# The first layer's down GEMM in a two-block kernel: four of its eight weight panels in three fp32r passes instead of fp32

## What is computed

```python
def rmsnorm(x, g):
    xf = x.astype(jnp.float32)
    y = xf * lax.rsqrt(jnp.mean(xf * xf, axis=-1, keepdims=True) + EPS)
    return (y * g.astype(jnp.float32)).astype(x.dtype)

def modulate_2(x, g, shift, scale):
    return rmsnorm(x, g) * (1 + scale) + shift

def conv_ffn(h, w_up, conv_w, conv_b, w_down, rows):
    u = h @ w_up
    ...                                   # depthwise convolution of u
    a, g = jnp.split(u, 2, axis=-1)
    return (jax.nn.silu(g) * a) @ w_down

# in second_block, for each layer:
mod_l = (jax.nn.silu(c) @ mod_w[layer] + mod_b[layer])[:, None, :]
...
xl = xl + g2l * conv_ffn(hl, ffn_w_up[layer], ffn_conv_w[layer], ffn_conv_b[layer], ffn_w_down[layer], rows)
xc = xc + g2c * conv_ffn(hc, ffn_w_up[layer], ffn_conv_w[layer], ffn_conv_b[layer], ffn_w_down[layer], None)
```

## Time and profile before

| | us |
|---|---|
| median of three runs | 2857.93 (2853.77 to 2861.48) |
| the profiled execution | 2861.58 |
| span of the profile | 2859.8 |
| PE busy | 2674.9 (94%) |
| DVE busy | 1931.4 (68%) |
| ACT busy | 1078.2 (38%) |
| POOL busy | 240.4 (8%) |

### The profile page before, as it was taken

One profiled execution on the slowest core, in us unless ns is written; L12 is line 12 of the kernel. 1 busy time (PEld: TensorE's weight loads), 2 busy tenths in 40 slices (PEclk: granted clock), 3 DMA queues, 4 the chain that ended last, 5 costly groups with the idle time before them and its releaser, 6 DMA issues.

```text
span 2859.8 us, 48632 instructions
## 1 busy us (share of the span) xinstructions
PE 2674.9 (94%) x18346; PEld 2282.1 (80%) x18346; DVE 1931.4 (68%) x3229; ACT 1078.2 (38%) x1387; POOL 240.4 (8%) x135
## 2 busy tenths in 40 slices
PE   3999999999999989999989999999999899989998
PEld 3998988899999888889967875787744677768887
DVE  6776656777778675575756743677777677764781
ACT  2434433443543433244464552433300645542211
POOL 0000000100000000000013310344300000000100
PEclk9999999999999999999999999999999999999999
DMA  8776734677677463445621211122367222123442
GB/s 304 267 279 225 289 124 157 240 275 265 231 270 269 162 225 118 146 176 182 245 73 63 76 45 45 63 99 88 110 259 294 81 88 74 61 73 125 155 160 76
DMA packets 105840, 468.66 MB, mean 164 GB/s; under 512 B 7004, under 2 KB 56744, under 8 KB 57784
## 3 DMA queue, kind: packets, MB, share of 16 engines
q1 hardware_dynamic: 105656, 466.18, 44.9%
HBM read 465.05 MB, written 1.06 MB: 163 GB/s over the span
## 4 chain that ended last, share of the span: by engine, by line
PE 49%; DVE 24%; DVEq 9%; ACT 7%; issue 5%; DMA 5%; ACTq 1%; SPq 1%; POOLq 0%
PE accs L702 7%; PE accs L703 7%; PE accs L704 7%; PE accs L687 7%; DVE panel_r L86 4%; DVEq L2951 4%; PE accs L842 4%; DVE arena L2928 3%; DMA panel<-w 2%; ACT arena L76 2%; DVE arena L2209 2%; DVE arena L86 2%; PE accs L1291 2%; PE accs L1009 2%; DVE cond_panel L2209 2%
## 5 line engine op out<-in xcount | busy, mean ns | idle before, releaser
L702 PE MATMUL accs<-normed_r,arena_r 128*128 128x256 f32 (+1 forms) x1832 | 573.8, 313 | 16.6 <-DVEq L2254 7.3
L703 PE MATMUL accs<-arena_r 128*128 128x256 f32 x2065 | 583.4, 283 | 0.0
L704 PE MATMUL accs<-normed_r,panel_r 128*128 128x256 f32 (+1 forms) x1840 | 572.1, 311 | 0.0
L86 DVE TENSOR_TENSOR panel_r<-panel,arena_r 128x1024 fp32r<-128x1024 f32 (+1 forms) x295 | 390.4, 1323 | 163.3 <-ACTq L1570 118.2
L1569 ACT ACTIVATE arena_r<-panel 128x1024 fp32r<-128x1024 f32 (+1 forms) x292 | 330.5, 1132 | 384.2 <-DMA panel<-w 137.4
L703 PEld LDWEIGHTS accs<-arena_r 128*128 128x128 f32 x2065 | 389.1, 188 | 1.0 <-issue 0.2
L702 PEld LDWEIGHTS accs<-normed_r,arena_r 128*128 128x128 f32 x1832 | 345.1, 188 | 52.3 <-issue 13.2
L704 PEld LDWEIGHTS accs<-normed_r,panel_r 128*128 128x128 f32 x1840 | 344.9, 187 | 22.3
L687 PE MATMUL accs<-normed,panel 128*128 128x256 f32 x1536 | 341.6, 382 | 5.3 <-ACT normed L76 2.4
L2928 DVE SCALAR_TENSOR_TENSOR arena<-accs,vectors,arena 128x189 f32<-128x189 f32 (+2 forms) x704 | 279.4, 428 | 96.3 <-issue 67.5
L687 PEld LDWEIGHTS accs<-normed,panel 128*128 128x128 f32 x1536 | 289.6, 190 | 51.7 <-issue 5.1
(11 more groups left out here) (426 smaller groups left out, 4648.7 us busy)
## 6 DMA issues: line engine op xcount, KB each, us to landing
panel<-w SPq DMA_DIRECT2D x250, 1024.0 KB, 4.9
panel<-w SPq DMA_DIRECT2D x48, 1408.0 KB, 8.0
cond_panel<-wc SPq DMA_DIRECT2D x57, 1024.0 KB, 6.3
normed<-wc SPq DMA_DIRECT2D x43, 1024.0 KB, 6.7
arena<-wc SPq DMA_DIRECT2D x19, 1024.0 KB, 4.9
residual<-xs SPq DMA_DIRECT2D x2, 1024.0 KB, 9.7
residual<-wc SPq DMA_DIRECT2D x1, 1024.0 KB, 13.2
residual<-crows SPq DMA_DIRECT2D x2, 512.0 KB, 9.1
```

The source lines that it names most:

```text
L86: i = self.eng.tensor_tensor(*a, **k)
L702: pe.matmul(out, hi[:, k, 0:m], src_hi(k), start=clear and k == 0, stop=False, skip_group_check=True)
L703: pe.matmul(out, hi[:, k, 0:m], src_lo(k), start=False, stop=False, skip_group_check=True)
L704: mm = pe.matmul(out, lo[:, k, 0:m], src_hi(k), start=False, stop=last and k == n - 1, skip_group_check=True)
```

## The change

1. `down0` becomes a split GEMM. Its part 1 panels (2, 3, 6, 7) are computed as three fp32r passes; part 0 panels (0, 1, 4, 5) stay fp32.
2. ACT, after the last hidden chunk, rounds hidden chunks 11 to 21 to fp32r (`wide_high`), and then makes the high parts of panels 2, 3, 6 and 7; those of 6 and 7 wait for the panels to land. All of this stands on ACT ahead of the squares of the norm.
3. DVE makes the low part of the same hidden chunks and the low parts of the four panels. The conditioning units are dealt anew: low parts of panels 2 and 3, units 0 to 7, n = 0, units 8 to 11, n = 1, low parts of panel 6, units 12 to 15, low parts of panel 7, units 16 to 23, n = 2, units 24 to 27, n = 3.
4. The squares of this norm lie in other places of memory (`squares3`), since the rounded hidden chunks lie where they were; so does the scratch output of the paired units.

```diff
-        order += [..., Gemm(f"down{l}", 8, both, wide=True, panels_per_acc=2, ahead=BANKS // both)]
+        order += [..., Gemm(f"down{l}", 8, both, wide=True, panels_per_acc=2, ahead=BANKS // both, split=(l == 0), kept=(l == 0))]
...
+        wide_hi = region(UC, KSPLIT, 512, of=arena_r)
+        wide_lo = region(KSPLIT * 512, KSPLIT, 512, of=arena_r)
...
@@ split_parts
+            if g.name == "down0":
+                hi = wide_w[(2 * u + j) % 4]
...
@@ PE, down
+                    if g.name == "down0" and part == 1:
+                        if n == 0:
+                            pe.wait_ge(S("wide_low"), 3)
+                        for j in range(2):
+                            b = (g.a0 + 2 * n + j) % BANKS
+                            split_half(g, 0, i, j, acc[b], lambda k: wide_hi[:, k, :], lambda k: wide_lo[:, k, :], False, True, ready[b])
+                        continue
...
@@ PE, POOL and ACT, the norm's squares
-                sq = squares2 if n in (2, 4) else squares
+                sq = (lambda k: squares3[k][:, 0:w]) if n == 2 else lambda k: (squares2 if n == 4 else squares)[:, k, 0:w]
...
@@ ACT, ffn_up
+                def wide_high():
+                    g = G["down0"]
+                    act.wait_ge(S("up_used"), 11)
+                    for c in (0, 4, 8):
+                        n = min(4, KSPLIT - c)
+                        act.activation(wide_hi[:, c:c + n, :], hid[:, KSPLIT + c:KSPLIT + c + n, :], ACT.Copy).then_inc(S("wide_high"), 1)
+                    for i in range(8):
+                        if i % 4 < 2:
+                            act.drain().then_inc(S("high_made"), 2)
+                        else:
+                            for j in range(2):
+                                if i >= 6:
+                                    wait_ready(act, g, 0, i - 6, j)
+                                high_kept(g, 0, i, j)
...
@@ DVE, add_branch
-                        for i in ((range(0, 10), range(10, 12), range(12, 24), range(24, 28))[u]):
+                        if u == 0:
+                            for c in (0, 4, 8):
+                                n = min(4, KSPLIT - c)
+                                dve.wait_ge(S("wide_high"), c // 4 + 1)
+                                dve.tensor_tensor(wide_lo[:, c:c + n, :], hid[:, KSPLIT + c:KSPLIT + c + n, :], wide_hi[:, c:c + n, :], ALU.subtract)\
+                                   .then_inc(S("wide_low"), 1)
+                        if u % 2 == 0:
+                            dve.drain().then_inc(S("low_made"), 4)
+                            for i in ((2, 3), (), (6,))[u]:
+                                low(g, 0, i)
+                        for i in ((range(0, 8), range(8, 12), range(12, 24), range(24, 28))[u]):
+                            if i == 16:
+                                low(g, 0, 7)
```

More of the change, by code:

```diff
@@ L158, in plan @@
             order += [Gemm("ssdout", 8, panels_per_acc=2, ahead=BANKS)]
-        order += [Gemm(f"up{l}", 22, both, split=(l == 0), kept=(l == 0)), Gemm(f"down{l}", 8, both, wide=True, panels_per_acc=2, ahead=BANKS // both)]
+        order += [Gemm(f"up{l}", 22, both, split=(l == 0), kept=(l == 0)), Gemm(f"down{l}", 8, both, wide=True, panels_per_acc=2, ahead=BANKS // both, split=(l == 0), kept=(l == 0))]
     p = a = splits = 0
@@ L309, in program @@
         pair_rows = [X[:, 4 * v:4 * v + 4, 0:T] for v in range(2)]
-        pair_again, pair_junk = [region(13312 + 1024 * v, 4, T) for v in range(2)], region(19456, 4, T)
+        pair_again, pair_junk = [region(13312 + 1024 * v, 4, T) for v in range(2)], region(22656, 4, T)
         hid = region(0, KF, 2 * T)
@@ L414, in program @@
         uconv = region(UC, 2, 4, 512)
+        wide_hi = region(UC, KSPLIT, 512, of=arena_r)
+        wide_lo = region(KSPLIT * 512, KSPLIT, 512, of=arena_r)
+        wide_w = [v.rearrange("p a b -> p (a b)")[:, i * KSPLIT * P:(i + 1) * KSPLIT * P].rearrange("p (k c) -> p k c", k=KSPLIT)
+                  for v in (sums_r[:, :, :], H_r[:, :, :]) for i in range(2)]
         squares2 = region(UC, KD, 2 * T)
+        squares3 = [region(UC + KSPLIT * 512 + 512 * k, 512) for k in range(3)] + \
+            [v[:, :, :].rearrange("p a b -> p (a b)")[:, 2816 + 512 * i:3328 + 512 * i] for v, i in ((sums, 0), (sums, 1), (H, 0), (H, 1))] + \
+            [region(UC, 512)]
         kept_hi = {"even": region(E_T, KD, PANEL, of=arena_r), "up0": region(UC + 4096, KD, PANEL, of=arena_r)}
@@ L506, in split_parts @@
         def split_parts(g, u, j):
-            if g.name in kept_hi:
+            if g.name == "down0":
+                hi = wide_w[(2 * u + j) % 4]
+            elif g.name in kept_hi:
                 hi = kept_hi[g.name][:, :, j * P:j * P + P]
@@ L891, in rms_norm @@
                     pe.wait_ge(S("rms_sq"), (n + 1) * KD + k + 1)
-                    mm = pe.matmul(mix[:, 0, 0:w], ones_d[:, :], sq[:, k, 0:w], start=(k == 0), stop=(k == KD - 1))
+                    mm = pe.matmul(mix[:, 0, 0:w], ones_d[:, :], sq(k), start=(k == 0), stop=(k == KD - 1))
                 mm.then_inc(S("rms_ready"), 1)
@@ L1515, in first_squares @@
             def first_squares(n, w):
-                sq = squares2 if n in (2, 4) else squares
+                sq = (lambda k: squares3[k][:, 0:w]) if n == 2 else lambda k: (squares2 if n == 4 else squares)[:, k, 0:w]
                 for k in range(1, 6):
                     pool.wait_ge(S("rms_sq"), (n + 1) * KD + k + 1)
-                    pool.tensor_tensor(sq[:, 0, 0:w], sq[:, 0, 0:w], sq[:, k, 0:w], ALU.add)
+                    pool.tensor_tensor(sq(0), sq(0), sq(k), ALU.add)
                     pool.drain()
@@ L1661, in rms_norm @@
                     act.wait_ge(S("rms_in"), (n - 1) * KD + k + 1)
-                    act.activation(sq[:, k, 0:w], X[:, k, sel], ACT.Square).then_inc(S("rms_sq"), 1)
+                    act.activation(sq(k), X[:, k, sel], ACT.Square).then_inc(S("rms_sq"), 1)
                 act.wait_ge(S("rms_ready"), n + 2)
@@ L1983, in body @@
                         silu(1 - par, it * 2 + (11 * l + par))
+                def wide_high():
[12 more added lines that the diff above has]
+                                high_kept(g, 0, i, j)
                 groups(act, g, body, peel=True)
                 silu(0, 11 * l + 11)
+                if l == 0:
+                    wide_high()
             act.wait_ge(S("row_loaded"), 16)
```

## The result

| | before | after |
|---|---|---|
| median, us | 2857.3 (2853.77 to 2861.48, 5 runs) | 2869.74 (2865.47 to 2874.41, 5 runs) |
| ratio after / before | | 1.0039, 95% interval 1.0026 to 1.0052 |
| the profiled execution, us | 2861.58 | 2874.41 |

A forecast was written before the change was run, and what follows sets the result against it. DVE with its transfers bounds the stage, not PE. 6.3 - 1.5 - 1.1 + 3.5 - 1.5 + 2.2 + 2.5 + 0.6 = +11.0 us, on a 2857.93 us median: forecast 2869 us, range 2861 to 2876.

The forecast's parts named there:

- What bounds: End of the down GEMM: DVE with its transfers decides, not PE; unit 27 is done 0.8 us after PE's turn.
- the rival for the faster side: End of the down GEMM: the last takeover waits for PE's last panel; -9.3 us, 2849 us; chance 0.06.
- PE's part: Four split panels: 15.3 us each instead of 18.92, 14.5 us less on PE, all off the path.
- waits for banks: PE ahead of panels 4 and 5: stands 3 us and some 3.5 us for accumulator banks, costing nothing.
- Start and first half: DVE to n = 1: unit 0 6.3 us late behind low parts; then -1.5 and -1.1, lateness 3.7 us.
- Panel 6 and unit 12: DVE: low parts of panel 6 +3.5, lateness 7.2; unit 12 without POOL's adds -1.5, lateness 5.7 us.
- Panel 7: DVE ahead of unit 16: low parts only partly hidden by the transfer wait; +2.2 us, lateness 7.9.
- POOL's adds: Units 16 and 17: three POOL adds slow DVE; +2.5 us, bounds 0 to 3.5, lateness 10.4.
- The norm: Norm behind the GEMM: PE's matmuls may run at 1.2 GHz after its long stand; +0.6 us, bounds 0 to 1.8.
- mostly hidden: Rival: panel 7's low parts fit the 3.98 us wait, POOL's adds fall into waits; about 2863 us; chance 0.23.
- Late landings: Dearer rival: panels 6 and 7 land late, POOL's adds and slow filler matmuls cost more; +15.7 us, 2874 us; chance 0.11.
- the filler: Part of the dearer rival: PE's filler matmuls at 1.2 GHz delay the next layer, +1.2 us from the norm.

The follow-up runs named there:

- all three edits: Kernel after plus third transfer slot, no POOL adds in this norm, and panel 7 issued behind unit 13: 2852.03 us, ratio 0.9984 to the kernel before.

## Why the prediction was right, step by step

- **What bounds.** Shown: 20 us added to PE moved the distance by 0.9 us, and taking the eleven subtracts away gave all of the loss back. That PE could decide was the rival for the faster side; it holds only in the kernel with a third slot and fp32 panels.
- **PE's part.** 15.3 us a panel, as predicted. (The working gave an fp32 panel 22 weight loads. It has 44: four panels with 66 instead raised the page's count of weight loads by 88, from 18346 to 18434. Nothing hung on it.) Its waits for banks were 3.14 us (3 predicted) and 1.68 (3.5 predicted). The second was too high because panel 4 took 1.6 us longer at a lower clock behind the first (last section), so that n = 1's takeover was nearer when PE came to it; none of this reached the end. PE was done at 2203.1 us (2203).
- **Start and first half.** 6.2 us at unit 0 for 6.3, 3.5 at the takeover of n = 1 for 3.7. The wait of unit 8 and the slow multiply under POOL's add went as worked out. The later experiment with more subtracts bears out that all of it is handed on.
- **Panel 6 and unit 12.** 7.2 for 7.2, and 6.1 for 5.7 at unit 14.
- **Panel 7, mis-sized.** Predicted +2.2, measured 9.1 - 6.1 = +3.0, and lateness 9.1 for 7.9 in all. I had put the panel's arrival by sharing the bytes between two landings, which gave 2172.2 us; it landed at 2172.98 (2163.73 + 9.25) and ACT copied from 2173.06. The panel was issued 5.5 us later than before (2158.26), as forecast, but took 9.25 us where my estimate meant 8.2 (before, it took 8.0). The size isn't fixed: 9.37 and 9.12 us with a fourth pass and with more subtracts, 7.88 without POOL's adds and 7.84 with a third slot. In the kernel with panel 7 issued sooner the stand for its copy is gone.
- **POOL's adds.** +2.7 for 2.5 between unit 16 and the last takeover: three multiplies, 3.1 us dearer, of which waits swallowed 0.4. For the kernel without adds I expected 4 us at most; less the 1.5 of panel 7's landing it gave 4.8.
- **The norm.** From the last takeover to the reciprocal it takes 6.07 us against 5.93 in this profile: +0.14, not +0.6. PE's clock was low there indeed; the columns of this window are its bounds, its length, busy time with count for PE, PE's weight loads, DVE, ACT and POOL, then PE's granted clock, DMA's busy share and GB/s:

```profile
2203.30:2226.00 22.70, 2.08 (x2) 0.50 (x2) 16.66 (x28) 1.26 (x2) 3.33 (x2) 0.55 0.79 303
```

A clock of 0.55 is nearly the lower level, 1.2 GHz, all through. The last four records of the sum took 3.44 us (2226.73 to 2228.60 + 1.57) for 3.30 before, which is the 0.14. The 3.30 us of before lay mostly at the lower level already, and here the clock rose again at 2229.7 us, ahead of their end. In five other kernels (fourth pass, no subtracts, third slot, no POOL adds, panel 7 sooner) the same stretch takes 6.41 us, +0.48. The last two of the four records in the kernel with a third slot show it, 1.91 us for 1.57:

```profile
2212.64 1.91 PE L916 MATMUL mix<-arena,ones_d 128*128 128x512 f32 x2
```

So the term was near what it is in most kernels, and small in this one profile. The two records of 2.08 us at 2213.74 run while DVE works.
- **Behind the stage, not predicted.** From the reciprocal to POOL's first add in the next layer it takes 370.4 us after and 368.5 before, +1.9; 0.8 of it is won back later, since the spans differ by 12.8. The windows of like place, before and then after, 38 us long and some 31 us behind the start of the reciprocal:

```profile
2250.00:2288.00 38.00, 34.44 (x177) 28.79 (x177) 28.62 (x39) 17.82 (x22) 0.00 (x0) 0.96 0.26 88
```

```profile
2262.00:2300.00 38.00, 34.42 (x169) 28.55 (x168) 28.36 (x39) 16.87 (x21) 0.00 (x0) 0.91 0.25 85
```

After, PE gets 169 matmuls done in the same busy time in which it got 177, at a mean clock of 0.91 for 0.96. The same distance was 368.4 us in the kernel with only new places and 368.5 in that with two panels, and 369.7 to 371.1 in the eight others; among these is the kernel before with a third slot (371.1), which has no three-pass panel. So it doesn't come from the three-pass panels as such. Each of the eight does show a lower clock than the two quick ones somewhere on this way, but not in one place: with all three edits it is the same 38 us (0.91), in the kernels without subtracts, with a third slot, without adds and with panel 7 sooner these stand at 0.96 as before and the last 248 us ahead of the add at 0.97 to 0.98 (0.99 before), with a fourth pass it is the first 31 us behind the start of the reciprocal (0.87), and in the last two (before with a third slot, more subtracts) these (0.89) and the 38 us behind them (0.91). That the clock makes the 1.9 us is argued from this and not shown by a run, and what starts it stays open.

The forecast's sum was +11.0 us; the profiled executions differ by 12.8, the medians by 12.4. The difference of 1.4 to 1.8 us is panel 7's landing (0.8 to 1.2) and this last piece, less what the norm took below its term. Both lie inside the range. That the median (2869.7) came within 1 us of the forecast is in part luck: the kernel before was now measured 0.6 us lower than the 2857.93 I started from, and the sum was 1.4 us short. Of the rivals, "mostly hidden" (2863 us) failed where it was said to be weak: panel 7 landed too late to be hidden. "Late landings" had panel 7 1.8 us dearer than the forecast, and 0.8 of it came; POOL's adds and the filler didn't grow as it had them. DVE's stand of 2.50 us for ACT's copy doesn't tell the two apart, since the forecast's own times gave one of 2.8 (unit 15 done at 2170.9, the copy at 2173.7).

## What to carry to other kernels

When an engine is fed through two slots and the next transfer starts only when it lets one go, don't count its idle time between units as room for more work. In this kernel the 5.2 us put ahead of them arrived at the end in full, though over the last 16 units the engine is idle for about a third of the time. First give the chain a third slot (13.2 us of the distance here), then add work to it, at the place where a real landing covers it, as the wait for unit 0 did. And before a faster form of matmul is bought with work on another engine, see which of the two ends last, and by how much. Here two converted panels, with a third slot and panel 7 sooner, brought the two level, and four, with POOL's adds gone as well, got no further.

## What the runs showed of the hardware

- POOL's adds slow DVE's subtracts too. A subtract of 128x1408 that met an add took 2.48 us (1.63 beside it without one), a multiply of 128x1024 2.31 us instead of 1.22. The Trainium skill (GPSIMD Engine Reference, Specifications) says that VectorE instructions with two SBUF inputs contend with POOL; the kernel before showed it for multiplies alone, and the trace with panel 7 sooner agrees for subtracts.
- Panel 7's transfer of 1408 KB took 9.25 us with units in flight beside it, and 7.84 to 9.37 in four other kernels. The order of the issues alone doesn't set it: the kernel without POOL's adds has the order of the kernel after and took 7.88. A unit's 1024 KB took 4.95 to 5.11 us in the undisturbed rounds.
- Behind the stand of 3.14 us for a bank PE's granted clock was 0.61 over 2131 to 2135 us (1.2 GHz for most of it), then 1.00, and panel 4 took 20.61 us instead of 18.96 (row below, columns as above). Before, PE stood 1.30 us at this place and went on with 13 records in 5.82 us, 0.45 each, at a granted clock of 1.00. The 1.6 us were off the chain here.

```profile
2131.00:2135.00 4.00, 3.89 (x6) 1.88 (x7) 3.51 (x7) 0.00 (x0) 0.00 (x0) 0.61 0.64 246
```

- With 23.9 us of PE mostly standing (2205.8 to 2229.7), the granted clock was at the lower level all the time; before, there were 3.4 us of it at 2216.1. It cost 0.14 us on the chain here, and 0.48 in five other kernels: only four records were waited for.
